# One step fewer per chain in the woven RWKV recurrence

## The chip, the cores and the metric

The kernel runs on one core of one Trainium2 chip. The metric is the device time of one execution in microseconds (us). A core has a matrix engine (TensorE, PE in the rows; its weight loads are PEld), a vector engine (VectorE, DVE), a scalar engine (ScalarE, ACT), a general one (GpSimd, POOL) and a queue for transfers (SyncE, SP). Each engine works through its own list of instructions in the order in which it was written; engines meet only at semaphores.

## The reference, cut to what matters

A two-layer block with latent attention, a bidirectional RWKV recurrence and a mixture of experts is followed by a second block with three attention branches and a convolutional feed-forward. The change lies in the recurrence of the first block, which runs twice (once per layer). For each of 8 heads and for both directions in time it computes

```
def step(S, inp):
    r_t, w_t, k_t, v_t, kk_t, b_t = inp
    sa = einsum('bhvk,bhk->bhv', S, kk_t)
    S = S * w_t[:, :, None, :] - sa[..., None] * b_t[:, :, None, :] + v_t[..., None] * k_t[:, :, None, :]
    return S, einsum('bhvk,bhk->bhv', S, r_t)
```

over 528 tokens, with a state S of 64 by 64 per head. All numbers are float32.

## The kernel before, in words

The function `wkv` cuts the 528 tokens into 11 chunks of 48 (`WC`), and a chunk in one direction is a chain: 22 chains, forward and backward by turns. Within a chunk the recurrence is a triangular system. A chain builds the inverse of its 48 by 48 matrix level by level, then solves with it, updates the state and adds to the output.

A chain has phases, and the generator `woven` writes them out: at step s every chain c whose phase p = s - 4c lies in 0 to 15 gets its phase, the oldest chain first. Chains start 4 steps apart (`GAP`), so four chains are under way and each fourth step looks alike. Every engine's list is written by the same generator, and each engine skips the phases for which it has no work. The vector engine's list has one difference: `woven(last=STEPS - 1)` puts the last phase (the state update) behind all other phases of its step.

What the phases do, by the line of the profile:

- 0: POOL writes the sides, an identity and half of uv; ACT takes exponentials (L1409 to L1416); DVE scales the sides (L1581 to L1584). No matrix work.
- 1: PE crosses the sides (L1475) and turns them (L1484); DVE masks the product (L1589); ACT keeps the turned ones (L1432).
- 2: PE turns the matrix (L1491). DVE grafts level 0: two predicated copies from SBUF (L1598), then one from PSUM (L1603).
- 3, 5, 9, "spreads": PE L1500; ACT copies 3 and 9 out (L1436), DVE copies 5 out with a mask (L1608).
- 4, 6, 7, 8, 10, 11, "grafts": PE L1515, with L1512 ahead of it in 4 and 8; DVE merges the product into the inverse by a predicated copy (L1615 for 4 and 8, L1621 for the others). The next spread or graft of the chain waits for that copy.
- 12: nothing on any engine.
- 13, "right side": PE L1525 and L1528; ACT keeps it (L1440).
- 14, "solve": PE L1536; ACT keeps it in two copies (L1446).
- 15, "state": PE L1542, L1545 and L1549; DVE updates the state (L1628, L1631) and adds to the output (L1636).

So the four steps of a period hold, oldest chain first: 8, 4, 0 | 13, 9, 5, 1 | 14, 10, 6, 2 | 15, 11, 7, 3. On DVE the last of them reads 11, 7, 15, since ACT takes 3. A block of 8 float32 matmuls stands in the rows as x16 (two records each); the 8 transposes of L1484 stand as x8.

Of the kernel before, what the change touches and what calls it, by code (L numbers as in the profile page):

```python
# [50 lines left out]
WN = T // WC  # L51
# [1205 lines left out]
def wkv(k, a, r, key, v, kk, sig, rate, y):  # L1257
# [7 lines left out]

    nc, ps = k.nc, k.ps
    R = WC + N_B
    CHAINS, STEPS, GAP, RING = 2 * WN, 16, 4, 4
    SPREAD_AT, GRAFT_AT = (3, 5, 9), (4, 6, 7, 8, 10, 11)
    BOTH, BAND_OF = (4, 8), {4: 1, 6: 2, 7: 2, 8: 2, 10: 4, 11: 4}  # L1270
    GRAFTS, SPREADS = 1 + len(GRAFT_AT), 1 + len(SPREAD_AT)
    with ExitStack() as tmp:
# [24 lines left out]
        def cut(t, c):  # L1297
            return t[:, :, chunk(c) * WC:(chunk(c) + 1) * WC]
# [29 lines left out]
        with k.stage("y_cleared", "cleared", "side_blank", "v_turned", "v_kept", "uv_set", "keyed", "decays", "staged", "paired",  # L1328
# [73 lines left out]
            @block.scalar  # L1402
            def _(act):
                def decay(c):
                    z, d = c % RING, c % 2
                    if c >= 2:
                        act.wait_ge(staged, c - 1)
                        act.wait_ge(paired, c - 1)
                    act.activation(e_neg[d][:, :, :], cut(sig[d], c), ACT.Exp,  # L1409
                                   scale=DECAY).then_inc(decays, 1)  # L1410
                    act.activation(e_pos[d][:, :, 1 - d:1 - d + WC], cut(sig[d], c), ACT.Exp,
                                   scale=-DECAY).then_inc(decays, 1)
                    if c >= RING:
                        act.wait_ge(state_kept, c - RING + 1)
                    end = 0 if d else WC - 1
                    act.activation(e_end[z][:, :, :], cut(sig[d], c)[:, :, end:end + 1], ACT.Exp,  # L1416
                                   scale=-DECAY).then_inc(decays, 1)
                for c in range(2):
                    decay(c)
                for n in range((WN + 1) // 2):  # L1420
                    act.wait_ge(v_turned, n + 1)
                    act.activation(v_tok[:, 2 * n:2 * n + 2, :].rearrange("p c n -> p (c n)"),
                                   ps[0:R, n, :], ACT.Copy).then_inc(v_kept, 1)
                for c, p in woven():
                    z, d, n = c % RING, c % 2, c // RING
                    if p == 0:
                        if c >= 2:
                            decay(c)
                    elif p == 1:
                        for b, bank in enumerate((bank_b(c, 1), bank_a(c + 1))):  # L1430
                            act.wait_ge(turned, 2 * c + b + 1)
                            act.activation(tok[z][:, b, :, :].rearrange("p f n -> p (f n)"),  # L1432
                                           ps[0:R, bank, 0:RT * N_B], ACT.Copy).then_inc(tok_kept, 1)
                    elif p in (3, 9):
                        act.wait_ge(x_made[z], SPREADS * n + 2 + SPREAD_AT.index(p))
                        act.activation(nt[z][:, :, :], ps[0:R, bank_a(c), 0:RT * WC].rearrange(  # L1436
                            "p (f n) -> p f n", f=RT), ACT.Copy).then_inc(x_kept[z], 1)
                    elif p == 13:
                        act.wait_ge(right, c + 1)
                        act.activation(rn[d][:, :, :].rearrange("p f n -> p (f n)"),  # L1440
                                       ps[0:R, bank_b(c, 0), 0:RT * N_B], ACT.Copy,
                                       scale=-1.0).then_inc(right_kept, 1)
                    elif p == 14:
                        act.wait_ge(solved, c + 1)
                        for b in range(2):
                            act.activation(uv[z][OWN[b], b, :, :].rearrange("p f n -> p (f n)"),  # L1446
                                           ps[OWN[b], bank_b(c, 1), 0:RT * N_B], ACT.Copy).then_inc(u_kept, 1)

            @block.tensor
            def _(pe):  # L1450
# [10 lines left out]
                for c, p in woven():  # L1461
# [32 lines left out]
                    elif p in SPREAD_AT:  # L1494
                        pe.wait_ge(grafted[z], GRAFTS * n + grafts_before(p))
                        if p == SPREAD_AT[-1]:
                            pe.wait_ge(far_made[z], 2 * n + 2)
                        for f, b, hb, hw in heads():
                            cross = far[d][hw, f, :] if p == SPREAD_AT[-1] else by[b][z][hw, f, 0, :]
                            last = pe.matmul(ps[hw, a0, f * WC:(f + 1) * WC], lhsT=cross,  # L1500
                                             rhs=inv[z][hw, 0, f, :], start=True, stop=True)
                        last.then_inc(x_made[z], 1)
                    elif p in GRAFT_AT:
                        if p in (4, 10):
                            pe.wait_ge(x_kept[z], 2 * n + (4, 10).index(p) + 1)
                        elif p == 6:
                            pe.wait_ge(x_cut[z], n + 1)
                        else:
                            pe.wait_ge(grafted[z], GRAFTS * n + grafts_before(p))
                        if p in BOTH:  # L1510
                            for f, b, hb, hw in heads():
                                pe.matmul(ps[hw, a0, f * WC:(f + 1) * WC], lhsT=inv[z][hw, 1, f, :],  # L1512
                                          rhs=nt[z][hw, f, :], start=True, stop=True)
                        for f, b, hb, hw in heads():
                            last = pe.matmul(ps[hw, a0, (RT + f) * WC:(RT + f + 1) * WC], lhsT=nt[z][hw, f, :],  # L1515
                                             rhs=inv[z][hw, 1, f, :], start=True, stop=True)
                        last.then_inc(y_made[z], 1)
                    elif p == 13:
                        pe.wait_ge(masked, 2 * min(c + 3, CHAINS))
                        if c >= 2:  # L1520
                            pe.wait_ge(state_kept, c - 1)
                            pe.wait_ge(y_kept, c - 1)
                        pe.wait_ge(uv_set, 4 * c + 4)
                        for f, b, hb, hw in heads():
                            pe.matmul(ps[hw, b0, f * N_B:(f + 1) * N_B], lhsT=kaprho[z][hb, f, 0, :],  # L1525
                                      rhs=state[d][hb, f, :], start=(f == 0), stop=False)
                        for f, b, hb, hw in heads():
                            last = pe.matmul(ps[hw, b0, f * N_B:(f + 1) * N_B], lhsT=by[b][z][:, f, 0, :],  # L1528
                                             rhs=uv[z][:, b, f, :], start=False, stop=(f == RT - 1))
                        last.then_inc(right, 1)  # L1530
                    elif p == 14:
                        pe.wait_ge(tok_kept, 2 * min(c + 3, CHAINS))
                        pe.wait_ge(right_kept, c + 1)
                        pe.wait_ge(grafted[z], GRAFTS * (n + 1))
                        for f, b, hb, hw in heads():
                            last = pe.matmul(ps[hw, b1, f * N_B:(f + 1) * N_B], lhsT=inv[z][hw, 1, f, :],  # L1536
                                             rhs=rn[d][hw, f, :], start=True, stop=True)
                        last.then_inc(solved, 1)
                    elif p == 15:
                        pe.wait_ge(u_kept, 2 * c + 2)  # L1540
                        for f, b, hb, hw in heads():
                            pe.matmul(ps[hb, b1, f * WC:(f + 1) * WC], lhsT=state[d][hb, f, :],  # L1542
                                      rhs=kaprho[z][hb, f, 1, :], start=(f == 0), stop=False)
                        for f, b, hb, hw in heads():
                            last = pe.matmul(ps[hb, b0, f * N_B:(f + 1) * N_B], lhsT=tok[z][:, b, f, :],  # L1545
                                             rhs=uv[z][:, b, f, :], start=True, stop=True)
                        last.then_inc(grown, 1)
                        for f, b, hb, hw in heads():
                            last = pe.matmul(ps[hb, b1, f * WC:(f + 1) * WC], lhsT=uv[z][:, b, f, :],  # L1549
                                             rhs=by[b][z][:, f, 1, :], start=False, stop=(f == RT - 1))  # L1550
                        last.then_inc(out_made, 1)

            @block.vector
            def _(dve):
# [17 lines left out]
                for c, p in woven(last=STEPS - 1):  # L1572
# [38 lines left out]
                    elif p in GRAFT_AT:  # L1611
# [8 lines left out]
                        else:  # L1620
# [1 line left out]
                                inv[z][0:R, 1, :, :], k.level[0:R, level, d + 1, None, :].to_broadcast([R, RT, WC]),  # L1622
                                ps[0:R, a0, RT * WC:2 * RT * WC].rearrange("p (f n) -> p f n", f=RT)
                            ).then_inc(grafted[z], 1)
                    elif p == 15:
                        dve.wait_ge(grown, c + 1)
                        dve.wait_ge(out_made, c + 1)
                        chain(dve.tensor_tensor(state[d][:, :, :], state[d][:, :, :],  # L1628
# [2772 lines left out]
```

## Time and profile before

| what | value |
|---|---|
| median of 3 runs | 3392.68 us (3379.67 to 3408.02) |
| the profiled execution | 3398.73 us, its span 3396.9 us |
| PE busy | 3009.3 us (89%), weight loads 2304.0 us |
| DVE busy | 1764.2 us (52%) |
| ACT busy | 844.7 us (25%) |
| POOL busy | 608.0 us (18%) |
| mean granted TensorE clock | 0.941 |
| the recurrence, layer 0 | about 337 to 566 us of the span |
| the recurrence, layer 1 | about 1316 to 1547 us |

Busy time is the time in which an engine had an instruction under way. Matmuls overlap, so their lengths add up to more than the time they take together; what a block costs is read from its start to the start of the next block. A bracket such as [0.42 <-PE ps L1515] is idle time of that engine just before the row, and who ended it.

### The profile page before, as it was taken

What the parts mean: (1) busy time and instruction counts of PE and PEld (TensorE: products, weight loads), DVE (VectorE), ACT (ScalarE), POOL (GpSimd) and SP (SyncE); (2) the same over time, 40 slices, a digit from 0 to 9 for tenths busy, and PEclk for the clock granted to TensorE, in tenths of its full rate; (3) what the DMA queues carried; (4) which work ended last, traced back from release to release, by engine and by line L of the source; (5) the groups of instructions that cost most, each with busy time, mean ns of one, the idle gap of its engine ahead of it and who ended that gap; (6) DMA issues with size and microseconds to landing.
All of it is one profiled execution on the core that took longest, in us unless ns stands there. A gap on an engine that the chain in (4) does not pass through costs nothing. (4 is left out here: it accounts for less than half of the span.)

```text
span 3396.9 us, 66987 instructions
## 1 busy us (share of the span) xinstructions
PE 3009.3 (89%) x27674; PEld 2304.0 (68%) x27674; DVE 1764.2 (52%) x3364; ACT 844.7 (25%) x1780; POOL 608.0 (18%) x915
## 2 busy tenths in 40 slices
PE   6998999968758998999588759999989999899998
PEld 3776898645436776997454434676566788688887
DVE  3445677431133455775511154455477776577742
ACT  3123232221131123331321141333543201121210
POOL 0001773011110004770111020000155100000000
PEclk9999899979978997999799969999999999999999
DMA  7111202099982203002599971101100122222220
GB/s 255 44 38 63 119 4 90 20 364 383 406 277 68 62 29 150 5 4 88 198 365 396 365 232 50 40 26 32 58 1 13 63 100 87 75 75 87 84 93 35
DMA packets 171509, 419.71 MB, mean 124 GB/s; under 512 B 30113, under 2 KB 116513, under 8 KB 145745
## 3 DMA queue, kind: packets, MB, share of 16 engines
q1 hardware_dynamic: 152241, 381.49, 30.2%
q0 software_dynamic: 8736, 17.32, 2.1%
q10 hardware_dynamic: 10240, 16.79, 1.5%
q8 instruction: 211, 3.46, 0.4%
q14 instruction: 81, 0.66, 0.1%
HBM read 398.82 MB, written 50.54 MB: 132 GB/s over the span
## 5 line engine op out<-in xcount | busy, mean ns | idle before, releaser
L2292 PE MATMUL ps<-e_w,e_xt 128*64 128x256 f32 x1792 | 233.5, 419 | 69.9 <-DMA e_w<-in_moe_w 68.5
L2292 PEld LDWEIGHTS ps<-e_w,e_xt 128*64 128x64 f32 x1792 | 153.8, 152 | 170.9 <-issue 82.1
L2399 DVE TENSOR_TENSOR e_hid<-ps,e_silu 64x256 f32<-64x256 f32 x64 | 39.4, 615 | 398.7 <-ACT e_silu L2358 398.7
L795 PE MATMUL ps<-h,win 128*128 128x264 f32 x960 | 224.9, 388 | 11.2 <-DVE pad L977 9.6
L795 PEld LDWEIGHTS ps<-h,win 128*128 128x128 f32 x960 | 179.7, 190 | 46.6 <-issue 17.2
L1515 PE MATMUL ps<-inv,nt 48*48 48x48 f32 x4224 | 135.2, 211 | 5.5 <-issue 5.4
L3837 PE MATMUL ps<-h_lat,wt 128*128 128x256 f32 x528 | 127.7, 384 | 6.7 <-ACT h_lat L3976 6.5
L3837 PE MATMUL ps<-h_lat,w_sums 128*128 128x256 f32 x544 | 129.5, 381 | 0.0
L2311 PE MATMUL ps<-e_w,e_hid_t 128*64 128x512 f32 x448 | 111.1, 614 | 15.2 <-DMA e_w<-in_moe_w 10.4
L1515 PEld LDWEIGHTS ps<-inv,nt 48*48 48x48 f32 x4224 | 117.7, 127 | 9.2 <-issue 6.1
L2362 ACT ACTIVATE e_hid_t<-ps 128x128 f32<-128x128 f32 x64 | 17.8, 278 | 403.9 <-PE ps L2300 403.9
L3837 PEld LDWEIGHTS ps<-h_lat,wt 128*128 128x128 f32 x528 | 100.8, 192 | 23.7 <-issue 7.9
L3837 PEld LDWEIGHTS ps<-h_lat,w_sums 128*128 128x128 f32 x544 | 104.3, 192 | 14.6
L977 DVE COPY pad<-ps 128x264 f32<-128x264 f32 x60 | 25.9, 432 | 167.0 <-PE ps L795 167.0
L3942 ACT ACTIVATE part<-ps 128x256 f32<-128x256 f32 x54 | 20.8, 384 | 355.4 <-PE ps L3837 262.0
L3837 PE MATMUL ps<-y_branch,wt 128*128 128x256 f32 x448 | 107.7, 379 | 0.8 <-ACT ff_up L3984 0.8
L1101 POOL MEMSET v<- 128x128 f32 x2 | 0.4, 208 | 550.0 <-POOLq L159 550.0
L3041 PE MATMUL ps<-wc,h_lat 128*128 128x256 f32 x384 | 91.7, 383 | 4.3 <-DVE log_f L3154 3.3
L3837 PEld LDWEIGHTS ps<-y_branch,wt 128*128 128x128 f32 x448 | 85.0, 190 | 13.1 <-ACT ff_up L3984 1.6
L1621 DVE COPY_PREDICATED inv<-level,ps 112x192 f32<-112x192 int32 x176 | 64.3, 373 | 53.8 <-PE ps L1515 53.7
L3303 POOL TENSOR_TENSOR c_e<-c_e,fg_bound 128x512 f32<-128x512 f32 x6 | 7.4, 1264 | 420.3 <-DMA fg_bound<-bounds 420.3
L3837 PE MATMUL ps<-ff_up,wt 128*128 128x256 f32 x336 | 81.2, 379 | 0.0
(675 smaller groups left out, 6869.4 us busy)
## 6 DMA issues: line engine op xcount, KB each, us to landing
e_w<-in_moe_w SPq DMA_DIRECT2D x168, 1024.0 KB, 12.5
early<-in_moe_w SPq DMA_DIRECT2D x24, 1024.0 KB, 12.3
wt<-in_w_up SPq DMA_DIRECT2D x22, 1024.0 KB, 5.0
y_rows<-e_y ACTq DMA_DIRECT2D x128, 128.0 KB
win<-in_w_in SPq DMA_DIRECT2D x10, 1536.0 KB, 6.7
wmod<-in_w_mod SPq DMA_DIRECT2D x24, 512.0 KB, 14.6
wt<-in_w_in SPq DMA_DIRECT2D x11, 1024.0 KB, 4.9
early<-in_w_mod SPq DMA_DIRECT2D x16, 512.0 KB, 11.2
```

Source lines behind the costliest of these rows:

```text
L795: last = pe.matmul(ps[:, 7, 0:HT], lhsT=ring[(s + 1) % 2][:, i, o:o + P], rhs=k.h[:, i, h * HT:(h + 1) * HT], start=(i == 0), stop=(i == K ...
L977: dve.tensor_copy(pad[:, 1 + h * HT:1 + (h + 1) * HT], ps[:, 7, 0:HT]).then_inc(emptied, 1)
L1515: last = pe.matmul(ps[hw, a0, (RT + f) * WC:(RT + f + 1) * WC], lhsT=nt[z][hw, f, :], rhs=inv[z][hw, 1, f, :], start=True, stop=True)
L1621: dve.copy_predicated(inv[z][0:R, 1, :, :], k.level[0:R, level, d + 1, None, :].to_broadcast([R, RT, WC]), ps[0:R, a0, RT * WC:2 * RT * WC ...
L2292: last = pe.matmul(ps[half, 2 + z, 0:EH], lhsT=xt[z][:, f, :], rhs=w[:, f, :], start=(f == 0), stop=(f == KD - 1))
L2311: last = pe.matmul(ps[half, 4 + z, :], lhsT=hid_t[z][:, t, :], rhs=m2[:, t, q * 512:(q + 1) * 512], start=(t == 0), stop=(t == 1))
L2362: act.activation(hid_t[z][:, :, :], ps[:, 2 + z, EH:EH + 2 * SLOT].rearrange("p (t n) -> p t n", t=2), ACT.Copy).then_inc(hid_kept[z], 1)
L2399: dve.tensor_tensor(hid[z][high, :].rearrange("s (t q) -> s q t", t=2), ps[high, 2 + z, 0:EH].rearrange("s (q t) -> s q t", t=2), si[z][hi ...
L3041: last = pe.matmul(ps[:, 7, 0:cols], lhsT=lhsT, rhs=rhs, start=(i == 0), stop=(i == KD - 1))
L3303: gp.tensor_tensor(lift_of(r, d), lift_of(r, d), bound[:, 0, d, :], ALU.mult).then_inc(lifted, 1)
L3837: last = pe.matmul(out, lhsT=w[:, i, :], rhs=x[:, i, :], start=(i == 0), stop=(i == w.shape[1] - 1))
L3942: act.activation(part[j % 2][:, 0, :], bank(j, 0)[:, 0:H], ACT.Copy).then_inc(p1_kept, 1)
```

## The change

The chain gets 15 phases instead of 16. The empty phase 12 is dropped: the right side moves from 13 to 12, the solve from 14 to 13, the state from 15 to 14, on every engine that has a part in them. Nothing is added or removed otherwise, and `woven(last=STEPS - 1)` still names the state phase. The four steps of a period then hold: 12, 8, 4, 0 | 13, 9, 5, 1 | 14, 10, 6, 2 | 11, 7, 3, where 12 is the right side, 13 the solve, 14 the state. On DVE the third reads 10, 6, 2, 14 and the fourth 11, 7.

```diff
-    CHAINS, STEPS, GAP, RING = 2 * WN, 16, 4, 4
+    CHAINS, STEPS, GAP, RING = 2 * WN, 15, 4, 4
...
             def _(act):
...
-                    elif p == 13:
+                    elif p == 12:
                         act.wait_ge(right, c + 1)
...
-                    elif p == 14:
+                    elif p == 13:
                         act.wait_ge(solved, c + 1)
...
             def _(pe):
...
-                    elif p == 13:
+                    elif p == 12:
                         pe.wait_ge(masked, 2 * min(c + 3, CHAINS))
...
-                    elif p == 14:
+                    elif p == 13:
                         pe.wait_ge(tok_kept, 2 * min(c + 3, CHAINS))
                         pe.wait_ge(right_kept, c + 1)
                         pe.wait_ge(grafted[z], GRAFTS * (n + 1))
...
-                    elif p == 15:
+                    elif p == 14:
                         pe.wait_ge(u_kept, 2 * c + 2)
...
             def _(dve):
...
-                    elif p == 15:
+                    elif p == 14:
                         dve.wait_ge(grown, c + 1)
                         dve.wait_ge(out_made, c + 1)
```

## Rows read from the trace of the kernel before

**Rows 1.** The page's first line: the span of the profiled execution.
```profile
span 3396.9 us, 66987 instructions
```

**Rows 2.** Windows: busy time of each engine (x instructions), clock, DMA share, GB/s.
```profile
core 0: us, PE busy (x) PEld busy (x) DVE busy (x) ACT busy (x) POOL busy (x), PEclk, DMA share, GB/s
520.00:548.00 28.00, 27.63 (x950) 26.02 (x947) 22.44 (x55) 8.69 (x27) 17.42 (x29) 1.00 0.02 5
```

**Rows 3.** Timeline of PE, one steady period: start, length, engine, line, tiles, count.
```profile
532.64 0.65 PE L1536 MATMUL ps<-rn,inv 48*48 48x64 f32 x16
533.13 0.88 PE L1515 MATMUL ps<-inv,nt 48*48 48x48 f32 x32
533.85 0.53 PE L1491 MATMUL ps<-ident,by 48*48 48x48 f32 x16
534.21 0.64 PE L1542 MATMUL ps<-kaprho,state 64*64 64x48 f32 x16
...
535.84 0.92 PE L1515 MATMUL ps<-inv,nt 48*48 48x48 f32 x32
536.60 0.53 PE L1500 MATMUL ps<-inv,by 48*48 48x48 f32 x16
537.24 0.56 PE L1512 MATMUL ps<-nt,inv 48*48 48x48 f32 x16
...
537.99 0.53 PE L1512 MATMUL ps<-nt,inv 48*48 48x48 f32 x16
...
538.71 0.62 PE L1525 MATMUL ps<-state,kaprho 64*48 64x64 f32 x16
...
539.84 0.56 PE L1500 MATMUL ps<-inv,far 48*48 48x48 f32 x16
540.24 0.53 PE L1500 MATMUL ps<-inv,by 48*48 48x48 f32 x16
540.74 1.03 PE L1475 MATMUL ps<-kaprho,side 64*112 64x96 f32 x16
...
541.92 0.65 PE L1536 MATMUL ps<-rn,inv 48*48 48x64 f32 x16
```

**Rows 4.** Timeline of DVE, the same period.
```profile
533.70 0.73 DVE L1621 COPY_PREDICATED inv<-level,ps 112x192 f32<-112x192 int32 x2 [0.19 <-PE ps L1515]
534.33 1.31 DVE L1598 COPY_PREDICATED inv<-level,by 48x192 f32<-48x192 int32 x2
535.66 0.37 DVE L1603 COPY_PREDICATED inv<-level,ps 112x192 f32<-112x192 int32 x1
536.45 0.73 DVE L1621 COPY_PREDICATED inv<-level,ps 112x192 f32<-112x192 int32 x2 [0.42 <-PE ps L1515]
537.09 0.41 DVE L1628 TENSOR_TENSOR state<-state,ps 128x256 f32<-128x256 f32 x1
...
537.88 0.34 DVE L1636 TENSOR_TENSOR y<-y,ps 128x192 f32<-128x192 f32 x1
538.21 1.31 DVE L1615 COPY_PREDICATED inv<-level,ps 112x384 f32<-112x384 int32 x2
539.41 0.54 DVE L1581 TENSOR_TENSOR side<-side,e_neg 128x384 f32<-128x384 f32 x1
...
540.14 0.35 DVE L1584 TENSOR_TENSOR kaprho<-u,e_pos 128x192 f32<-128x192 f32 x1
```

**Rows 5.** Timeline of DVE one period later, when POOL has no sides left.
```profile
543.61 1.03 DVE L1598 COPY_PREDICATED inv<-level,by 48x192 f32<-48x192 int32 x2
```

**Rows 6.** Timeline of ACT in the steady period: the two copies of the solve.
```profile
533.34 0.78 ACT L1446 ACTIVATE uv<-ps 48x256 f32<-48x256 f32 x2
```

**Rows 7.** Timeline of PE at the start of layer 0's recurrence, no state phase yet.
```profile
358.47 0.89 PE L1515 MATMUL ps<-inv,nt 48*48 48x48 f32 x32
360.16 0.56 PE L1500 MATMUL ps<-inv,by 48*48 48x48 f32 x16 [0.80 <-DVE inv L1603]
```

**Rows 8.** Timeline of PE some ten us later: an idle stretch and what follows.
```profile
372.12 1.44 PE L1515 MATMUL ps<-inv,nt 48*48 48x48 f32 x30 [2.07 <-issue]
```

**Rows 9.** Windows: layer 1's recurrence, columns as in Rows 2.
```profile
1316.00:1548.00 232.00, 216.44 (x6864) 201.79 (x6864) 161.65 (x393) 67.46 (x215) 161.42 (x279) 0.94 0.12 48
```

## The prediction, made before the changed kernel ran

> **What bounds the recurrence now.** I took the windows first: in 28 us of the steady stretch PE is busy 27.63 and DVE 22.44, at full clock [rows 2]. So PE sets the pace, but DVE has only a fifth of the time free, and an engine in that position becomes the bound as soon as its work comes at the wrong moment. Then the timelines of one period. It runs from solve to solve, 532.64 to 541.92, that is 9.28 us per chain [rows 3]. I read what each PE block costs from its start to the next start: solve 0.49, grafts 10 and 6 0.72, turn (2) 0.36, state 1.63, grafts 11 and 7 0.76, spread 3 0.36 (the same 16 records as the turn), graft 8 0.75, graft 4 0.72, right side 1.13, spread 9 0.40, spread 5 0.36, cross and turn (1) 1.18. They add up to 8.86. The other 0.42 is idle: 0.28 between the end of spread 3 (536.60 + 0.36) and graft 8 at 537.24, and 0.14 ahead of phase 1 at 540.74.
>
> The DVE timeline says why the first stands there: the copies of grafts 11 and 7 end at 536.45 + 0.73 = 537.18, and graft 8 starts 0.06 later [rows 3, 4]. I take 0.06 as the way from DVE to PE. The other way, block 11 ends at 535.84 + 0.38 = 536.22 and DVE starts at 536.45, block 10 ends at 533.49 and DVE starts at 533.70: I take 0.22.
>
> **What the change removes.** No instruction of any engine: phase 12 was empty, so an empty step costs nothing on an in-order list. The count of steps falls from 100 to 99 (4 x 21 + 15), but a step is not a unit of time. What changes is only the order: on PE the state block (1.63) now stands before graft 10 and no longer before graft 11, the solve (0.49) before 9 and no longer before 10, the right side (1.13) before 8 and no longer before 9. On DVE the state update stands between the level-0 graft of phase 2 and grafts 11 and 7, where it used to follow them. No DMA is issued in these phases, and SP has nothing in them.
>
> **The new period, walked through from the rows.** Time 0 is the start of the state block, now the first of its step.
>
> - PE: state to 1.63, graft 10 to 1.99, 6 to 2.35, turn to 2.71, 11 to 3.09, 7 to 3.47.
> - DVE gets graft 10 at 1.99 + 0.22 = 2.21 and copies 10 and 6 in 0.73, to 2.94. Then the two L1598 copies, then L1603 (0.37) [rows 4].
> - L1598's pair has two prices: 1.33 up to L1603's start while POOL works on sides [rows 4], 1.03 when POOL had no sides left [rows 5]. After the change it falls beside POOL's filling of uv and far, lighter than the sides but not idle. I take 1.20, between them, and keep both for the range. DVE is then done at 4.51.
> - PE may start spread 3 at 4.57. It was free at 3.47. **New wait: 1.10.** Before, the state block lay between turn and 11 and covered just this: L1603 ended at 536.03, spread 3 started at 536.60, so 0.57 was to spare, and 1.63 of cover is taken away.
> - Spread 3 to 4.93, right side to 6.06. DVE meanwhile does the state update (537.09 to 538.22, so 1.13 [rows 4]), 4.51 to 5.64, and only then 11 and 7, to 6.37. Graft 8 starts at 6.43. **Wait: 0.37**, where it was 0.28: the right side's cover is spent on the state update that has moved ahead of the copies.
> - Graft 8 to 7.18, graft 4 to 7.90, solve to 8.39, spread 9 to 8.79, spread 5 to 9.15. DVE copies 8 from 7.40 and 4 from 8.12 (0.60 each, 538.21 to 539.41 for two), to 8.72, just in time for spread 5.
> - DVE's phase 0 takes 1.08 (539.41 to 540.49) and ends at 9.80, so phase 1 starts at 9.86. **Wait: 0.71**, where it was 0.14, because the short solve stands where the long right side stood. This step has an uncertain latency: before, phase 1 started 0.25 after DVE's end, though it may just have been the PE's own change of block. Taking 0.25 instead of 0.06 adds 0.19.
> - Phase 1 to 11.04, and the next state block follows.
>
> The period is 11.04 instead of 9.28, **1.76 more**. With 1.03 for L1598 it is 10.87 (1.59 more), with 1.33 and the longer latency 11.36 (2.08 more). ACT has room: the solve ends at 8.39, its copies take 0.78 [rows 6] and are needed at 11.04. POOL's uv waits for the state and solve blocks, which come no later than before relative to their use, so I cost it at nothing; its cover is the free time that it has, 10.58 of 28 us [rows 2], which a longer period stretches. Were it gone, every 0.1 us by which POOL ends late would stand ahead of DVE's L1581 and cost 3.8.
>
> The best evidence that this is no artefact of my arithmetic is in the ramp. There no state block exists yet, so the PE order there is already the new one, 10, 6, turn, 11, 7, 3, and spread 3 waits 0.80 for DVE inv L1603 [rows 7]. The state update is not in DVE's way there and graft 10 does not wait behind a state block, so it gives a second value for the first wait; with 0.80 for 1.10 the period would be 10.74, 1.46 more. I stay with the walk and let this be the low end.
>
> **The sum.** The new order bites where a state phase meets a younger chain's phase 3: chains 3 to 21, 19 per layer, 38 in both. 38 x 1.76 = 67 us. Ends: 38 x 1.46 = 55 and 38 x 2.08 = 79. At ramp and drain I cost nothing, since the same blocks stand there; I allow 3 us per layer either way, because the drain has its own waits. The profiled execution took 3398.7 us with a span of 3396.9 [rows 1], some 6 us above the median of 3392.7, so a profile of the changed kernel would be about 3466 and the median about **3460**.
>
> A page speaks against this reading. The Trainium skill's "Perfetto Trace Analysis", section "Identifying the Most-Contended Engine", says to improve the engine with the highest occupancy. By it PE, with nothing added and its gaps the only thing to gain, would not get slower here; its time is that of the first rival below. No number of mine uses it.
>
> **The rivals.**
>
> 1. *The right side covers graft 8, and nothing else gets late.* For: the 0.28 wait is real, and 1.13 of work moves just in front of it. It decides if DVE finishes the level-0 graft less than about 0.28 after PE has issued graft 7, at 3.75 in my walk; the rows put it at 4.51, and the ramp shows the wait. Price: 38 x 0.28 = 11 less, 3382; with both waits gone 38 x 0.42 = 16 less, 3377. That would be within 1%, not slower. Chance 0.06. It is the case in which the page's rule holds.
> 2. *The step count is what counts.* One step of 9.28 / 4 = 2.3 us less in each layer: 5 us less, 3388. Against: phase 12 puts nothing in any list. Chance 0.04.
> 3. *The waits cost the clock.* After 2.07 us idle PE comes back with 1.44 us for 30 records, against 0.88 for 32 at full clock [rows 3, 8], and layer 1's recurrence has a mean of 0.94 [rows 9]. If repeated waits of 1.1, 0.4 and 0.7 brought the granted clock from 2.4 to 1.2 GHz, blocks would take 0.048 / 0.0275 = 1.75 times as long, 8.86 x 1.75 = 15.5 per period and 38 x 6.2 = 236 more, 3629; in a quarter of the periods it would add some 43 to my sum, 3503. Against: the ramp's wait of 0.80 left the blocks at full speed, 0.56 for spread 3 [rows 7]. Chance 0.05.
> 4. *Part of the waits only.* DVE has more slack than I give it, for instance if L1598 runs ahead of its place or the wait before phase 1 does not appear: 38 x (1.76 - 0.57) = 45, 3438. Chance 0.10.
>
> **How the numbers follow.** My case has 0.75. Its own range is 3448 to 3472, plus the scatter of the runs of before (13 below the median, 15 above). With case 4 taken in below and the light end of case 3 above I give 3430 to 3490; outside lie cases 1 and 2 and most of 3, about 0.15. A change of this kernel's time under 1% (34 us) can hardly be told from none. Slower by over 1% means above 3427: my case, 3 and nearly all of 4, 0.88. Within 1%: cases 1, 2 and the rest, 0.11. Faster by over 1% would need 34 us, and PE's idle time in these periods is 16 us in all: 0.01.
>
> **What would show it.** In the changed profile: a period of 10.8 to 11.3 us between two solve blocks; a bracket of about 1.1 ahead of L1500 released by DVE inv L1603, in nearly every period; DVE L1628 ahead of the L1621 pair of 11 and 7; a wait of about 0.7 ahead of L1475; PE busy in the windows down to some 80%, with the clock unchanged. The recurrence would be longer by about 33 us in each layer, and everything outside it the same. A period near 9.2 without the bracket at L1603 would make me wrong at the first wait; a short wait there with L1475 punctual, at the third; blocks of 0.9 in place of 0.5 would mean the clock.

## The result, and the profile after

The changed kernel takes 3440.78 us (median of 4 runs, 3433.27 to 3446.85) against 3390.68 us (median of 4, 3379.67 to 3408.02) for the kernel before: 50 us more. The ratio is 1.0139, with a 95% interval from 1.0108 to 1.0170. The ratio is not that of the two medians: it gives 47 us, and the experiments below are given by it. The kernel is slower by over 1%, as forecast, and its time lies inside the range, 19 us below the point forecast of 3460.

A window of the steady stretch of layer 0 and one of most of the recurrence of layer 1, kernel after (columns as in [rows 2]):

```profile
520.00:548.00 28.00, 24.73 (x826) 23.13 (x820) 18.25 (x47) 7.85 (x25) 19.01 (x34) 1.00 0.02 4
1340.00:1590.00 250.00, 215.52 (x6780) 199.71 (x6778) 152.76 (x387) 66.97 (x214) 153.87 (x275) 0.96 0.11 42
```

PE is busy 24.73 of 28 us, where it was 27.63 [rows 2]. DVE too has fallen, from 22.44 to 18.25: both wait more, for each other. The clock is 1.00 in the steady stretch, as before; the 0.96 of the second row comes from low stretches at the two ends of that recurrence, before 1373 and after 1580 us.

One period on PE, kernel after, from a solve to the next:

```profile
530.52 0.62 PE L1536 MATMUL ps<-rn,inv 48*48 48x64 f32 x16
...
531.38 0.56 PE L1500 MATMUL ps<-inv,by 48*48 48x48 f32 x16
532.55 1.03 PE L1475 MATMUL ps<-kaprho,side 64*112 64x96 f32 x16 [0.61 <-DVE kaprho L1584]
...
533.73 0.67 PE L1542 MATMUL ps<-kaprho,state 64*64 64x48 f32 x16
...
535.39 0.92 PE L1515 MATMUL ps<-inv,nt 48*48 48x48 f32 x32
...
536.51 0.89 PE L1515 MATMUL ps<-inv,nt 48*48 48x48 f32 x32
537.91 0.56 PE L1500 MATMUL ps<-inv,by 48*48 48x48 f32 x16 [0.51 <-DVE inv L1603]
538.30 0.62 PE L1525 MATMUL ps<-state,kaprho 64*48 64x64 f32 x16
538.85 0.65 PE L1528 MATMUL ps<-uv,by 112*48 112x64 f32 x16
539.71 0.56 PE L1512 MATMUL ps<-nt,inv 48*48 48x48 f32 x16 [0.21 <-DVE inv L1621]
...
541.18 0.62 PE L1536 MATMUL ps<-rn,inv 48*48 48x64 f32 x16
```

All three waits of the prediction are there, each with the releaser that it named. A bracket starts at the modelled end of the last matmul; counted from where the next block could have started, with the block lengths of [rows 3], the waits are 0.64 before spread 3 (536.51 + 0.76 = 537.27 to 537.91), 0.28 before graft 8 (538.85 + 0.58 = 539.43 to 539.71) and 0.81 before phase 1 (531.38 + 0.36 = 531.74 to 532.55). The period is 10.66 us.

DVE in the same period, kernel after:

```profile
536.00 0.74 DVE L1621 COPY_PREDICATED inv<-level,ps 112x192 f32<-112x192 int32 x2 [1.40 <-PE ps L1515]
536.64 0.83 DVE L1598 COPY_PREDICATED inv<-level,by 48x192 f32<-48x192 int32 x2
537.48 0.37 DVE L1603 COPY_PREDICATED inv<-level,ps 112x192 f32<-112x192 int32 x1
537.75 0.41 DVE L1628 TENSOR_TENSOR state<-state,ps 128x256 f32<-128x256 f32 x1
538.20 0.64 DVE L1631 TENSOR_TENSOR state<-state,e_end 128x256 f32<-128x256 f32 x1
...
539.03 0.62 DVE L1621 COPY_PREDICATED inv<-level,ps 112x192 f32<-112x192 int32 x2
540.68 1.30 DVE L1615 COPY_PREDICATED inv<-level,ps 112x384 f32<-112x384 int32 x2 [1.02 <-PE ps L1515]
541.88 0.54 DVE L1581 TENSOR_TENSOR side<-side,e_neg 128x384 f32<-128x384 f32 x1
```

The state update stands ahead of the copies of grafts 11 and 7, and DVE idles 1.40 behind the state block. What is not as forecast is one length: the pair of L1598 takes 0.84 (536.64 to 537.48), where it took 1.33 [rows 4].

I read the starts of all 22 solve blocks in each layer, from one trace of each kernel. From the second solve to the nineteenth there are 17 periods per layer. Before, they are not all 9.28: they run from 9.27 to 10.01, mean 9.48 and 9.54. After, all but the first of layer 0 (13.0, with a granted clock of 0.50 up to 386 us) lie between 10.66 and 10.68. From first cross product to last solve the recurrence goes from 224.3 and 226.5 us to 247.8 and 246.9, 43.9 more in both layers together. That is the size of the measured 47 to 50 us, but it is not a balance of one pair of traces: the spans of these two executions are 3396.9 and 3431.4 us, 34.5 apart, so what lies outside the recurrence was 9 us shorter in the second one. The times of one kernel scatter by as much (3379.67 to 3408.02 before the change).

### The profile page after: what moved, and what is told of

It reads as the page before. It is cut to its first block and busy times, and to the rows that moved or that the text cites. A ratio compares the mean times of both kernels' runs of the same rounds, so it can differ in the third digit from the quotient of the medians.

```text
span 3431.4 us, 66987 instructions
## 1 busy us (share of the span) xinstructions
PE 3005.4 (88%) x27674; PEld 2300.6 (67%) x27674; DVE 1750.1 (51%) x3364; ACT 842.4 (25%) x1780; POOL 603.7 (18%) x915
## 5 line engine op out<-in xcount | busy, mean ns | idle before, releaser
L1515 PEld LDWEIGHTS ps<-inv,nt 48*48 48x48 f32 x4224 | 114.8, 126 | 10.4 <-issue 6.1
L3837 PEld LDWEIGHTS ps<-h_lat,wt 128*128 128x128 f32 x528 | 100.9, 192 | 23.6 <-issue 7.9
L1615 DVE COPY_PREDICATED inv<-level,ps 112x384 f32<-112x384 int32 x88 | 51.8, 589 | 67.1 <-PE ps L1515 62.1
L1368 POOL TENSOR_TENSOR side<-kh,u 64x192 f32<-64x192 f32 x88 | 82.1, 933 | 6.9
## 6 DMA issues: line engine op xcount, KB each, us to landing
early<-in_w_mod SPq DMA_DIRECT2D x16, 512.0 KB, 10.3
```

The lines of the kernel that those rows point to most:

```text
L1368: gp.tensor_tensor(side[d][rows, :, OTHER[b]], kh[d][rows, :, :], cut(key, c)[rows], ALU.mult).then_inc(keyed, 1)
L1615: dve.copy_predicated(inv[z][0:R, :, :, :], k.level[0:R, level, d:d + 2, None, :].to_broadcast([R, 2, RT, WC]), ps[0:R, a0, 0:2 * RT * WC] ...
L3837: last = pe.matmul(out, lhsT=w[:, i, :], rhs=x[:, i, :], start=(i == 0), stop=(i == w.shape[1] - 1))
```

## The experiments

Each is compared with the kernel before, run between its own runs on the same chip. "Over" is the ratio's excess times some 3393 us. The recorded expectations count from medians: their 50 for the changed kernel and their 88 for the first run below are 47 and 85 in the table. Where a kernel is built on the changed one, 47 over means no effect. The period is the most frequent one of the steady stretch; the kernel before has 9.27 to 10.01.

| kernel | period, us | over, us (95% interval) | ratio |
|---|---|---|---|
| changed kernel | 10.67 | 47 (37 to 58) | 1.0139 |
| state update behind grafts 11, 7 | 10.4 to 14.9 | 85 (73 to 97) | 1.0251 |
| level-0 copies early | 9.94 | 20 (12 to 27) | 1.0059 |
| state block last on PE | 9.88 | 18 (11 to 26) | 1.0054 |
| right side alone moved | 10.13 (four of 34 at 10.4 to 11.4) | 32 (20 to 43) | 1.0093 |
| scaling first | 10.52 | 37 (28 to 45) | 1.0108 |
| level-0 copies early, on before | 9.28 to 10.1 | -1 (-8 to 5) | 0.9996 |
| level 0 and scaling | 9.80 | 8 (2 to 15) | 1.0025 |
| all three | 9.79 | 8 (3 to 14) | 1.0024 |
| level 0, scaling, GpSimd turned round | 9.37 | 1 (-4 to 6) | 1.0004 |
| all three, GpSimd turned round | 9.37 | -6 (-12 to 0) | 0.9983 |
| state update late, GpSimd turned round | 10.86 | 52 (39 to 65) | 1.0154 |
| GpSimd turned round, on before | 9.28 to 9.8 | 2 (-7 to 10) | 1.0005 |

**State update behind the copies of grafts 11 and 7, VectorE alone.** (`woven` also takes the number of steps here.)

```diff
-                for c, p in woven(last=STEPS - 1):
+                for c, p in woven(last=STEPS, steps=STEPS + 1):
...
-                    elif p == 14:
+                    elif p == 15:
                         dve.wait_ge(grown, c + 1)
```

> The changed kernel, with one thing moved back on VectorE alone: its state update (L1628 to L1636) stands behind the copies of grafts 11 and 7 again, one step later than on TensorE. Theory A (three separate TensorE waits for VectorE make up the loss: 0.65 us before spread 3, 0.28 before graft 8, 0.81 before phase 1): the wait before graft 8 goes, the other two stay, the period falls from 10.66 to about 10.35, 38 x 0.3 = 11 us less, so about 39 us over the kernel before instead of 50. Theory B (VectorE has simply become the bound by its total work per period): the same work in another order, 50 us over. Theory C (only the state block missing as cover before graft 11 on TensorE counts): also 50 us over.

Measured: 3479.45 us, 85 over. All theories missed the time. The wait before graft 8 went, as theory A said, and eleven of 36 periods in the two layers have its length, 10.30 to 10.44 us against 10.35. In the others the scaling of phase 0 ran beside GpSimd's side products. PE in a period of the first kind and in one of the second:

```profile
513.02 1.03 PE L1475 MATMUL ps<-kaprho,side 64*112 64x96 f32 x16 [0.61 <-DVE kaprho L1584]
...
524.18 1.03 PE L1475 MATMUL ps<-kaprho,side 64*112 64x96 f32 x16 [1.38 <-DVE kaprho L1584]
...
525.97 1.08 PE L1545 MATMUL ps<-uv,tok 112*64 112x64 f32 x16
526.82 1.05 PE L1549 MATMUL ps<-by,uv 112*64 112x48 f32 x16
```

DVE of the same kernel, in the second kind of period:

```profile
522.08 0.62 DVE L1581 TENSOR_TENSOR side<-side,e_neg 128x384 f32<-128x384 f32 x1
522.62 0.74 DVE L1583 TENSOR_TENSOR kaprho<-kk,e_pos 128x192 f32<-128x192 f32 x1
523.28 0.65 DVE L1584 TENSOR_TENSOR kaprho<-u,e_pos 128x192 f32<-128x192 f32 x1
```

L1583 takes 0.74 instead of 0.35 and the wait grows from 0.61 to 1.38, which makes a period of 11.15 us. The two go together: up to 530 us the bracket is 0.61 in each period in which L1583 takes 0.35 and 1.36 to 1.39 in each in which it takes 0.74. Here the blocks behind it, which took 0.69 and 0.62, take 1.08 and 1.05: the granted clock is 0.50 from 526.1 to 529.4 us. Periods in which that happens last 12.6 to 14.9 us. Over the 36 periods the longer waits add 18 us and the low clock 28 more (estimates, from the lengths of the periods and the brackets). The window of the steady stretch, kernel with the late state update:

```profile
400.00:540.00 140.00, 123.25 (x3666) 116.47 (x3662) 88.66 (x209) 36.47 (x120) 82.23 (x152) 0.88 0.01 4
```

A mean clock of 0.88, where every other kernel has 1.00 in this window: part of the stretch runs at the lower of the two levels, 1.2 instead of 2.4 GHz. The third rival of the prediction is real on this chip, though not in the changed kernel, whose steady stretches stay at 1.00.

**Level-0 copies at the end of phase 1.**

```diff
-                    elif p == 2:
                         dve.wait_ge(inv_set, c + 1)
                         dve.wait_ge(masked, 2 * c + 2)
...
+                    elif p == 2:
                         dve.wait_ge(x_made[z], SPREADS * n + 1)
```

> The changed kernel, with the two level-0 copies of L1598 moved on VectorE from phase 2 to the end of phase 1, where it idles 1.4 us per period. Theory A: the 0.65 us before spread 3 goes, the one before graft 8 shrinks from 0.28 to about 0.2, the 0.81 before phase 1 stays; period about 9.9, 38 x 0.75 = 29 us less, so about 21 us over the kernel before. Theory B (VectorE's total work): no change, 50 us over. Theory C (missing cover of the state block): the cover is still missing but there is less to cover, as theory A for this wait.

Measured: 3411.94 us, 20 over, period 9.94. The wait before spread 3 is gone, 0.19 before graft 8 and 0.61 (bracket) before phase 1 remain. Theory A said 21 over and 9.9. The run excludes B: VectorE does the same work.

**State block last in its step on TensorE alone.**

```diff
             def _(pe):
...
-                for c, p in woven():
+                for c, p in woven(last=STEPS - 1):
```

> The changed kernel, with one thing moved on TensorE alone: in its step the state block comes last, behind grafts 10 and 6 and the turn, so that it lies before graft 11 again; VectorE, ScalarE and GpSimd keep their lists. Right side and solve stay where the change put them. Theory A: the waits before spread 3 and graft 8 go, the 0.81 before phase 1 stays, and the turn waits some 0.24 for VectorE's masks, since 1.66 us of cover is gone from there; period about 9.9, some 22 us over the kernel before. Theory C alone (all of the loss is the state block's place): no loss left, 0 us over or less. Theory B: 50 us over.

Measured: 3413.37 us, 18 over, period 9.88. Of the 47 us, 29 go with the state block's place; 18 stay, and in the trace they are the wait before phase 1 and a wait of 0.20 that the turn now has for VectorE's masks. Theory C alone is out.

**Right side alone moved, 16 steps.**

```diff
-                    elif p == 13:
+                    elif p == 12:
                         act.wait_ge(right, c + 1)
...
-                    elif p == 13:
+                    elif p == 12:
                         pe.wait_ge(masked, 2 * min(c + 3, CHAINS))
```

> The kernel before with 16 steps, and only the right side moved one step earlier, to the empty phase 12; solve and state stay. Theory A: graft 8's 0.28 us wait goes, but phase 1 waits about 0.8 for VectorE's scaling (L1581 to L1584), and spreads 9 and 5 some 0.15 and 0.3, as the 1.13 us of the right side no longer lie before them: period about 10.0 to 10.2, 27 to 35 us over the kernel before. Theory C (the loss is all in the state block's place): 0.28 x 38 = 11 us below the kernel before. Theory B: 0 us.

Measured: 3426.92 us, 32 over, period 10.13, as theory A said. PE, the right side alone moved:

```profile
522.32 0.56 PE L1500 MATMUL ps<-inv,by 48*48 48x48 f32 x16 [0.15 <-DVE inv L1615]
523.49 1.03 PE L1475 MATMUL ps<-kaprho,side 64*112 64x96 f32 x16 [0.61 <-DVE kaprho L1584]
```

Graft 8 no longer waits, but phase 1 does. Filling the one wait that PE had gives 0.28 us and still makes the period 0.85 longer than 9.28, with the step count untouched: 16 steps here, 15 in the run before it. The loss does not need a smaller count. In layer 1 of this kernel one period has a low clock too, 0.50 from 1504.2 to 1507.4 us, behind brackets of only 0.32 and 0.61:

```profile
1502.51 0.56 PE L1500 MATMUL ps<-inv,by 48*48 48x48 f32 x16 [0.32 <-DVE inv L1615]
1503.68 1.44 PE L1475 MATMUL ps<-kaprho,side 64*112 64x96 f32 x16 [0.61 <-DVE kaprho L1584]
```

**Scaling ahead of the copies of grafts 8 and 4.** (ScalarE's list gets `first=0` too.)

```diff
-                for c, p in woven(last=STEPS - 1):
+                for c, p in woven(last=STEPS - 1, first=0):
...
-                        dve.wait_ge(decays, 3 * c + 3)
+                        dve.wait_ge(decays, 3 * c + 2)
```

> The changed kernel, with VectorE's phase 0 (the scaling, L1581 to L1584) put ahead of the copies of grafts 8 and 4 in its step, and ScalarE's exponentials for it ahead of the right side's copy; the scaling no longer waits for the third exponential, which only the state update needs. Theory A (the loss is the sum of three TensorE waits for VectorE, each with its own remedy): the 0.81 us before phase 1 goes, the 0.65 before spread 3 and the 0.28 before graft 8 stay; period about 9.85, so about 20 us over the kernel before instead of 50. Theory B (VectorE's total work is the bound): 50 us over. Theory D (after the miss of the run that put the state update behind the grafts: what VectorE shares with GpSimd decides, and every move that brings the scaling beside GpSimd's side products makes it longer): the scaling takes 1.7 instead of 1.1 us and the gain is a third smaller.

Measured: 3438.42 us, 37 over, period 10.52. A gain of 10 us, where theory A said 30 and theory D some 20: both too high, D the nearer. The wait before phase 1 went, as A said, but VectorE's work grew. DVE, scaling first:

```profile
515.88 0.65 DVE L1584 TENSOR_TENSOR side<-side,e_neg 128x384 f32<-128x384 f32 x1
516.46 0.74 DVE L1586 TENSOR_TENSOR kaprho<-kk,e_pos 128x192 f32<-128x192 f32 x1
517.12 0.74 DVE L1587 TENSOR_TENSOR kaprho<-u,e_pos 128x192 f32<-128x192 f32 x1
517.79 1.05 DVE L1618 COPY_PREDICATED inv<-level,ps 112x384 f32<-112x384 int32 x2
```

(Its lines are three further down than in the kernel before.) The scaling takes 1.91 instead of 1.08, and the copy of graft 8, now behind it, is late for spread 9, by 0.29. The waits before spread 3 and graft 8 stay.

**Level-0 copies early, on the kernel before.** The edit of the second run, on 16 steps.

> The kernel before (16 steps), with the two level-0 copies of L1598 moved to the end of phase 1 as in the run on the changed kernel that gained 29 us. Theory A (the copies cost only where the state block no longer covers them): spread 3 did not wait, so nothing is gained, 0 us within 5. Theory B (VectorE's work is the bound in both orders): as much as on the changed kernel, 20 to 30 us less.

Measured: 3396.67 against 3398.03 us, ratio 0.9996 (0.9977 to 1.0015). The move that gains 27 us after the change gains nothing before it: the same copies, covered here by the state block and bare there.

**Level 0 and scaling together.** Both edits.

> The changed kernel with both moves on VectorE's list: the level-0 copies at the end of phase 1, the scaling ahead of the copies of grafts 8 and 4. Theory A: only a wait of about 0.2 us before graft 8 is left; period 9.05 against 9.28 before, 38 x 0.23 = 9 us below the kernel before. Theory B: 50 us over. Theory D: the scaling meets GpSimd's work and the period stays at 9.3 or above, no gain over the kernel before.

Measured: 3405.96 us, 8 over, period 9.80. Theory A is 17 us too low, theory D is right: the scaling met GpSimd's work, and there is no gain over the kernel before. A wait of 0.19 before graft 8 and one of 0.30 before spread 9 remain.

**All three moves on VectorE.**

> As the run before, with the state update on VectorE behind the copies of grafts 11 and 7 as well. Theory A: no wait left, period 8.9, 38 x 0.38 = 14 us below the kernel before. Theory D: the later state update pushes VectorE's two-input work beside GpSimd's side products again and the period is longer than in the run with two moves.

Measured: 3404.98 us, 8 over, period 9.79. Both theories missed: the period is neither 8.9 nor longer than with two moves. The wait before graft 8 went and the one before spread 9 grew from 0.30 to 0.56: on one engine's list, what comes forward pushes something back.

**GpSimd's list turned round, on the run with two moves.** The "far products" of this and the next texts are GpSimd's phase 5 (L1397), which masks `by` for spread 9.

```diff
+                    if p == (5 if c else 0):
                         if c >= RING:
                             gp.wait_ge(solved, c - RING + 1)
...
-                    elif p == 5:
+                    elif p == 9:
                         n = c // RING
                         gp.wait_ge(masked, 2 * c + 2)
```

> As the run with two moves (level-0 copies early, scaling ahead of grafts 8 and 4), and GpSimd's list turned round: it makes the side products of a chain while TensorE is in the state block, and then, beside VectorE's scaling, the lighter identity, zeros, copy of v and far products (a chain's filling and far products come one period later in its list). No work is added. Theory D (in the run with two moves the scaling took 1.91 us instead of 1.08 because it ran beside GpSimd's side products): L1586 and L1587 fall back towards 0.35 us, the 0.3 before spread 9 goes, the period falls from 9.80 to 9.1 to 9.3, 38 x 0.6 = 23 us less than the 8 over, so about 10 to 15 us below the kernel before. Theory A2 (the scaling is longer for another reason, such as its place behind the graft copies): the period stays at 9.80, 8 us over.

Measured: 3395.95 against 3394.72 us, 1 over, period 9.37. DVE of this kernel:

```profile
514.40 1.24 DVE L1601 COPY_PREDICATED inv<-level,by 48x192 f32<-48x192 int32 x2
...
518.41 0.83 DVE L1585 TENSOR_TENSOR side<-side,e_neg 128x384 f32<-128x384 f32 x1
519.16 0.65 DVE L1587 TENSOR_TENSOR kaprho<-kk,e_pos 128x192 f32<-128x192 f32 x1
519.73 0.34 DVE L1588 TENSOR_TENSOR kaprho<-u,e_pos 128x192 f32<-128x192 f32 x1
520.00 1.05 DVE L1619 COPY_PREDICATED inv<-level,ps 112x384 f32<-112x384 int32 x2
```

The scaling is down from 1.91 to 1.59, not to 1.08: GpSimd's far products and then its identity copy run beside L1585 and L1587, while L1588, beside a fill with zeros, takes its own 0.34. L1598's pair (L1601 here) now lies beside the side products and is up from 0.77 to 1.24. The direction is theory D's; the 10 to 15 us below the kernel before did not come.

**The same, on the run with three moves.**

> As the run before, with the state update on VectorE behind the copies of grafts 11 and 7 as well. Theory D: no wait before graft 8 either; period 8.9 to 9.2, 10 to 18 us below the kernel before. Theory A2: 7 us over, as the run with three moves.

Measured: 3387.49 against 3394.72 us, ratio 0.9983 (0.9966 to 1.0000), period 9.37. The 10 to 18 us of theory D did not come here either. By the two ratios it beats the changed kernel by 1.5%; over the kernel before, the gain is at the edge of what the runs can tell.

**Late state update, GpSimd turned round.** The first run's edit and that of GpSimd's list.

> The run that put VectorE's state update behind the copies of grafts 11 and 7 (88 us over the kernel before, where 39 was forecast), with GpSimd's list turned round as in the last two runs and nothing else. Theory E (that run lost twice: the scaling ran beside GpSimd's side products, the wait before phase 1 grew to 1.4 us, and after such a wait TensorE's granted clock fell to its lower level): the scaling goes back to about 1.3 us, the waits before phase 1 stay near 0.9, the clock in the steady stretch is 1.00 again instead of 0.88, period 10.3 to 10.6, 30 to 42 us over the kernel before. Theory F (a later state update is itself harmful, through the next chain that needs the state): as before, some 80 us over.

Measured: 3446.03 us, 52 over, period 10.86. Its steady window:

```profile
400.00:540.00 140.00, 119.87 (x4021) 112.35 (x4018) 96.89 (x233) 39.30 (x129) 83.92 (x169) 1.00 0.02 4
```

and, from one period, its rows of level 0 on DVE, of GpSimd beside it, of spread 3 and of the scaling:

```profile
513.35 0.59 POOL L1365 TENSOR_TENSOR side<-kk,rate 64x192 f32<-64x192 f32 x1
513.53 1.30 DVE L1599 COPY_PREDICATED inv<-level,by 48x192 f32<-48x192 int32 x2
...
515.27 0.56 PE L1501 MATMUL ps<-inv,by 48*48 48x48 f32 x16 [0.98 <-DVE inv L1604]
...
519.43 0.35 DVE L1584 TENSOR_TENSOR kaprho<-kk,e_pos 128x192 f32<-128x192 f32 x1
519.70 0.35 DVE L1585 TENSOR_TENSOR kaprho<-u,e_pos 128x192 f32<-128x192 f32 x1
```

Theory E: the clock is back, the scaling is back to its own length, and of the first run's 85 us 33 are gone. Its 30 to 42 us and its period of 10.3 to 10.6 were missed, since L1598's pair pays for the move: it stands beside the side products and takes 1.32 to L1603's start against 0.84 in the changed kernel, and the bracket ahead of spread 3 goes from 0.51 to 0.98. Theory F would have left 80.

**GpSimd turned round, on the kernel before.**

> The kernel before (16 steps), with GpSimd's list turned round alone. It tells whether that move gains by itself or only where it frees VectorE. Theory D: before, no TensorE wait hangs on a VectorE instruction that GpSimd lengthens, except that L1598's pair had 0.57 us to spare; nothing changes within 5 us. If GpSimd's place mattered in itself (its fill of uv late, for instance): 10 us or more in either direction.

Measured: 3394.02 against 3397.91 us, ratio 1.0005 (0.9980 to 1.0030). The medians differ by 4 us one way and the ratio by 2 the other, both within the interval: no gain by itself, as forecast.

## Why the prediction was right, point by point

**An empty step costs nothing; only the order changes.** Right. The instructions are the same 66987, and the run with 16 steps and the right side moved has the same wait before phase 1 (bracket 0.61) as the changed kernel with 15.

**First wait, before spread 3, forecast 1.10: 0.64.** The mechanism is shown by three runs: moving the copies off its path or the state block back into it removes the wait and 27 to 29 us, and on the kernel before the first of these moves gains nothing. The size was off by L1598's pair, for which I took 1.20 and which takes 0.84. I had bounded it below by 1.03, the shortest pair in my rows, and the bound did not hold. That pair, at 543.61 in the kernel before, had no side products beside it but the far products, as GpSimd's row there shows; in the changed kernel the pair has only the filling of uv beside it and takes 0.8:

```profile
542.93 1.48 POOL L1397 TENSOR_TENSOR far<-by,far_band 48x192 f32<-48x192 f32 x2 [3.85 <-DVE by L1589]
```

```profile
536.41 0.31 POOL L1384 MEMSET uv<- 48x256 f32 x1
536.78 0.46 POOL L1386 COPY uv<-v_tok 48x256 f32<-48x256 f32 x1
```

The two copies ahead of the pair also take 0.64 to the next start and not 0.73, since the recorded length of a VectorE instruction overlaps the next one by about 0.1 us. I had added lengths where starts were to be subtracted. The ramp's 0.80 was no second value in the same measure: it is a bracket, and counted from starts that wait was 0.93 (358.47 + 0.76 = 359.23 to 360.16 [rows 7]).

**Second wait, before graft 8, forecast 0.37: 0.28.** Right in cause: with the state update behind the copies the wait is gone from the trace. The size is near partly by luck: the state update takes 1.28 (537.75 to 539.03) and not 1.13, and the overlaps take back 0.2. The wait is as big as before the change, so the 1.13 us of right side that now stand in front of it gain nothing.

**Third wait, before phase 1, forecast 0.71: 0.81.** Right. The longer way from VectorE, 0.25, that I had held open was the true one: L1584 ends at 532.30 (the row is 531.94, 0.36 long) and phase 1 starts at 532.55, exactly as before the change. That adds 0.19 to the 0.71; the copies of grafts 8 and 4 take some of it back, 1.20 from start to start (540.68 to 541.88) where the walk had 1.32.

**The base.** The sum was made against a period of 9.28, read from a stretch where it is 9.28. Over 17 periods in each layer the kernel before has 9.51. So a period grew by 10.67 - 9.51 = 1.16 and not by 1.76: 0.37 of the difference is the walk, 0.23 the base. 38 x 1.16 = 44 meets the 43.9 of the two recurrences partly by luck. The 34 periods between the second and the nineteenth solve hold 41.8 of it, 2.3 of them in the one period of 13.0. The last three periods of a layer, which the sum puts at nothing, grew by 3.3 us each time (20.3 to 23.6), and what comes before the second solve shrank by about 2.2. The base was the cheapest error to avoid: one more view, all periods instead of one or two, would have shown it. But it is no fixed number either: the two other kernels with PE's order of before have means of 9.52 (level-0 copies early) and 9.35 (GpSimd turned round). What makes those periods longer is not settled; the gaps are a few tenths, at changing blocks, and the profile names no releaser ("issue"). They are absent from the changed kernel's steady stretch, where PE has waits in every period to absorb them.

**The rivals.** The first (right side covers graft 8 and nothing gets late) fails as its condition said: level 0 was done at 537.85, 0.58 after PE could have gone on. The prediction had read the Trainium skill, "Perfetto Trace Analysis", section "Identifying the Most-Contended Engine", as a forecast of the time, and that fails with it: the section says which engine to improve first, and not what a change of order costs. PE was that engine, no work was added to it, and the time still went up. The second is excluded by the measured time and by the run with 16 steps. The third did not decide here, but the late state update shows that it can. The fourth, part of the waits only, gave 3438 and is nearer to the measured 3441 than the 3460 of my own case, though no wait failed to appear: the first was 0.46 shorter than forecast, the second 0.09 shorter, the third 0.10 longer. The measured time lies in the range because the range took in case 4; my case alone, 3448 to 3472, reaches it only with the scatter of the runs.

**The signs.** As forecast: the three releasers, L1628 ahead of the copies of grafts 11 and 7, the wait ahead of L1475 (0.81 for about 0.7), the clock unchanged. Short of the forecast: the period (10.67 for 10.8 to 11.3), the bracket at L1603 (0.51 for about 1.1), PE's busy share (88% for some 80%) and the recurrence (23.4 and 20.4 us longer for 33).

**What I had for one pair only: GpSimd lengthens VectorE.** The prediction gave L1598's pair two prices and every other VectorE instruction one. Means over the same 140 us (400 to 540), kernel before:

```profile
L1615 DVE COPY_PREDICATED inv<-level,ps 112x384 f32<-112x384 int32 x30 | 17.7, 591 | 2.6 <-PE ps L1515 1.0
L1598 DVE COPY_PREDICATED inv<-level,by 48x192 f32<-48x192 int32 x30 | 17.1, 571 | 0.2
L1631 DVE TENSOR_TENSOR state<-state,e_end 128x256 f32<-128x256 f32 x15 | 6.4, 425 | 0.5
L1628 DVE TENSOR_TENSOR state<-state,ps 128x256 f32<-128x256 f32 x15 | 6.2, 413 | 0.0
```

and kernel after:

```profile
L1615 DVE COPY_PREDICATED inv<-level,ps 112x384 f32<-112x384 int32 x26 | 15.3, 589 | 15.0 <-PE ps L1515 13.3
L1598 DVE COPY_PREDICATED inv<-level,by 48x192 f32<-48x192 int32 x26 | 10.6, 408 | 0.2
L1631 DVE TENSOR_TENSOR state<-state,e_end 128x256 f32<-128x256 f32 x14 | 9.1, 649 | 0.5
L1628 DVE TENSOR_TENSOR state<-state,ps 128x256 f32<-128x256 f32 x13 | 5.4, 414 | 0.0
```

L1598 gets shorter and L1631 longer; L1615 and L1628, which have one input in PSUM, stay as they are. In the runs with the scaling moved, L1583 and L1584 double. All that change have both inputs in SBUF. That GpSimd does it, and not the place in VectorE's list, is shown by the two runs with the late state update, which differ in GpSimd's list alone: L1583 goes back from 0.74 to 0.35, and the pair of L1598 goes from 0.83 to 1.30. It is not always VectorE that is held up: in the changed kernel the scaling keeps its length (531.22 to 532.30), and GpSimd's L1368, which starts beside it at 531.20, takes 1.55 us where its other instructions of that kind take 0.59. The Trainium skill, "SBUF — State Buffer", section "Who interferes with whom", says this: a VectorE instruction with two SBUF inputs contends with a GpSimd instruction that reads SBUF, and one with at most one SBUF input does not, unless it runs in a mode that uses two ports. The trace agrees: 571 against 408 ns and 425 against 649 for the first kind, 591 against 589 and 413 against 414 for the second.

## What to carry to other kernels

A block of matrix work in a woven schedule is also the cover for what another engine must finish behind it, so filling an empty slot takes the cover from somewhere: list, for each block that moves, the wait it hides now and the copies that run under it, and how much they have to spare. Take the base period from all periods, subtract starts instead of adding lengths, and do not mix brackets with waits counted from starts. When an order on one engine is repaired, look at what its neighbour is reading at the new time: of the nine re-orderings of the changed kernel seven met the same contention at a new place, and none clearly beat the kernel before.

## What the runs showed of the hardware

**The granted clock behind short waits.** In the kernel with the late state update, 22 of 36 periods have a bracket of 1.36 to 1.39 us before phase 1. In eleven of these the granted clock went from 1.00 to 0.50, 0.7 to 2.0 us after the wait had ended, for 3.4 to 10.3 us at a time; no fall began in a period with a bracket of 0.61. The mean was 0.88 over 140 us, with PE busy 123.25 of them. The length of that wait alone does not decide it: eleven such waits had no fall behind them, one fall in the kernel with the right side alone moved came behind 0.32 and 0.61, and with 0.98 and 0.61 in nearly every period (late state update, GpSimd turned round) the steady stretches stayed at 1.00, as they did with the changed kernel's 0.51, 0.21 and 0.61. What does is left open. I had given that rival 5% on the ground of one wait of 0.80. A longer wait cost 0.8 us of a period (10.39 to 11.15), the clock 1.4 to 3.8 more, so a re-ordering that costs 39 us by the sum cost 85.

**Which instructions two engines make longer for each other.** With a GpSimd product beside them the VectorE instructions with two SBUF inputs took up to about twice as long (0.35 to 0.74 us, the pair of L1598 0.77 to 1.31); those with one input in PSUM kept their length (589 and 591, 413 and 414 ns).

**The way from VectorE to TensorE.** It was 0.06 us before spread 3 and graft 8 and 0.25 before phase 1, the same in both kernels where both have the wait. Why phase 1 takes longer is open.
